# Output projection in 24 tiles of 344 columns instead of 16 groups of 2 x 258, and some steps in another place

## What is computed

```python
hn = rmsnorm(h, norm_mix)
z = hn @ w_in                                    # 1024 -> 3584
u_in, c_gate, b_gate, q, k, v, g = split(z)
y_conv = b_gate * causal_conv3(c_gate * u_in, conv_w)
o, ret_state = retention(rotary(q), rotary(k) * QK_DIM ** -0.5, v)   # chunks of 128, 4 heads
y_ret = head_rmsnorm(o) * silu(g)
h = h + concat([y_conv, y_ret]) @ w_out          # output projection, 1024 -> 1024
hn2 = rmsnorm(h, norm_mlp)
h = h + square(relu(hn2 @ w_up)) @ w_down        # 1024 -> 4096 -> 1024
y = rmsnorm(h, norm_final)
```

## Time and profile before

| | us |
|---|---|
| median of 3 runs | 1154.47 |
| lowest, highest | 1154.11, 1156.49 |
| the profiled execution | 1154.86 |
| its span, first to last instruction | 1153.1 |
| PE busy | 1141.2 (99%) |
| DVE, POOL, ACT busy | 769.6, 557.7, 442.2 |
| output projection, first matmul to first of the next stage | 389.48 to 481.90 |

### The profile page before, as it was taken

One profiled execution on the slowest core, in us unless ns is written; L12 is line 12 of the kernel. 1 busy time (PEld: TensorE's weight loads), 2 busy tenths in 40 slices (PEclk: granted clock), 3 DMA queues, 4 the chain that ended last, 5 costly groups with the idle time before them and its releaser, 6 DMA issues.

```text
span 1153.1 us, 22631 instructions
## 1 busy us (share of the span) xinstructions
PE 1141.2 (99%) x8685; PEld 1120.0 (97%) x8685; DVE 769.6 (67%) x1147; ACT 442.2 (38%) x915; POOL 557.7 (48%) x540
## 2 busy tenths in 40 slices
PE   9999999999999999999999999999999999999996
PEld 7899999999999999999999999999999999999996
DVE  4355546456455576689777777776878777777856
ACT  6422413413324433453333333334553443544414
POOL 0154233252251240124233242322899899999992
PEclk9999999999999999999999999999999999999998
DMA  6431221311202042154534435336972544454314
GB/s 205 133 109 40 60 72 42 88 54 37 84 29 57 30 137 84 47 150 169 182 116 147 148 123 182 111 130 228 298 253 88 183 148 133 144 185 147 93 38 147
DMA packets 154296, 139.79 MB, mean 121 GB/s; under 512 B 6842, under 2 KB 118179, under 8 KB 154205
## 3 DMA queue, kind: packets, MB, share of 16 engines
q1 hardware_dynamic: 149071, 135.50, 36.8%
q10 hardware_dynamic: 5134, 3.05, 0.9%
HBM read 98.07 MB, written 40.47 MB: 120 GB/s over the span
## 4 chain that ended last, share of the span: by engine, by line
PE 97%; DMA 1%; DVE 1%; issue 0%; ACT 0%; SPq 0%; DVEq 0%; ACTq 0%
PE pair L1911 19%; PE pair L1912 18%; PE pair L1913 18%; PE pair L1695 8%; PE pair L1697 8%; PE pair L1696 8%; PE pair L1888 3%; PE pair L1890 3%; PE pair L1889 3%; PE pair L1754 1%; PE pair L1755 1%; PE pair L1757 1%; PE pair L1805 1%; PE pair L1800 1%; PE pair L1814 1%; PE pair L1802 1%
## 5 line engine op out<-in xcount | busy, mean ns | idle before, releaser
L1911 PE MATMUL pair<-m_hi,dn_hi 128*128 128x258 f32 (+2 forms) x896 | 255.3, 285 | 0.4 <-DVE hid L1663 0.3
L1911 PE MATMUL pair<-b_hi,up_hi 128*128 128x258 f32 x896 | 254.8, 284 | 0.0
L1912 PE MATMUL pair<-b_lo,up_hi 128*128 128x258 f32 x896 | 253.6, 283 | 0.0
L1912 PE MATMUL pair<-m_lo,dn_hi 128*128 128x258 f32 (+2 forms) x896 | 253.6, 283 | 0.0
L1913 PE MATMUL pair<-m_hi,dn_lo 128*128 128x258 f32 (+2 forms) x896 | 253.3, 283 | 0.0
L1913 PE MATMUL pair<-b_hi,up_lo 128*128 128x258 f32 x896 | 252.1, 281 | 0.0
L1695 PE MATMUL pair<-x_hi,w_both 128*128 128x344 f32 (+2 forms) x576 | 188.8, 328 | 0.0
L1697 PE MATMUL pair<-x_hi,w_both 128*128 128x344 f32 (+2 forms) x576 | 184.3, 320 | 0.0
L1696 PE MATMUL pair<-x_lo,w_both 128*128 128x344 f32 (+2 forms) x576 | 184.2, 320 | 0.0
L1663 DVE TENSOR_TENSOR hid<-pair,hid 128x516 f32<-128x516 f32 (+2 forms) x194 | 124.6, 642 | 76.4 <-PE pair L1913 74.3
L1911 PEld LDWEIGHTS pair<-b_hi,up_hi 128*128 128x128 f32 x896 | 169.2, 189 | 2.0 <-issue 0.2
(11 more groups left out here) (214 smaller groups left out, 2167.8 us busy)
## 6 DMA issues: line engine op xcount, KB each, us to landing
m_raw<-m_dram SPq DMA_DIRECT2D x56, 516.0 KB, 4.8
m_dram<-hid SPq DMA_DIRECT2D x64, 258.0 KB, 2.8
up_raw<-w_up_dram SPq DMA_DIRECT2D x32, 512.0 KB, 5.0
dn_raw<-w_down_dram SPq DMA_DIRECT2D x128, 128.0 KB, 2.4
w_raw<-w_in_dram SPq DMA_DIRECT2D x28, 512.0 KB, 3.7
m_dram<-hid SPq DMA_DIRECT2D x16, 774.0 KB, 4.0
h_dram<-hid SPq DMA_DIRECT2D x8, 516.0 KB, 3.1
h_in<-h_dram SPq DMA_DIRECT2D x16, 258.0 KB, 5.8
```

Of the source, the lines that this page charges most:

```text
L1911: m_.matmul(to, shs[k], mhs[k], start=STARTS[i] and k == 0, stop=False, skip_group_check=more)
L1912: m_.matmul(to, shs[k], mls[k], start=False, stop=False, skip_group_check=more)
```

## The change

The 16 groups become 24 tiles, three for each output block (`TILE_OUT`), each of 344 columns in a single bank; six banks (0 to 5) are used in turn. Tile 1 of a block crosses the border of the two halves of columns. Everything that counted groups counts tiles: `h_done` and `main_done`, and the waits on them. `tiles_of(gi)` gives the number of tiles that must be read before the steps of half-group gi. `out_read` adds one bank of 344 columns. `y_low` counts each of its pieces, and the first two tiles wait for the pieces one by one. DVE's order at the last block changes: the two `up_low` that stood before the last read stand before the last but one. Some steps elsewhere are moved: ACT's `m_hi` of products 5 and 6 in block 0 of MLP down; `scaled(LASTU, 3)` on DVE and `squared(LASTU, 3)` on ACT by one product; three parameter loads from ACT's queue to SP's; the meta rows in one load; one warm-up matmul fewer; the last store on ACT's queue.

```diff
+TILE_OUT = [(n, t) for n in range(KT) for t in ((0, 1, 2) if n < 4 else (2, 1, 0))]
+TILES = len(TILE_OUT)
...
-MID_HIGH = ({11: 0, 13: 1, 15: 2, 17: 3, 20: 4, 22: 5, 24: 6}, {4: 0, 6: 1, 8: 2, 12: 3, 15: 4, 19: 5, 22: 6})
+MID_HIGH = ({11: 0, 13: 1, 15: 2, 17: 3, 20: 4, 21: 5, 22: 6}, {4: 0, 6: 1, 8: 2, 12: 3, 15: 4, 19: 5, 22: 6})
...
-WARM = (8, 3)
+WARM = (7, 3)
...
-        def out_pair(gi):
-
-            return pair[gi % 3 if gi < 12 else 3 if gi == 12 else (gi - 1) % 3]
+        def tiles_of(gi):
+
+            return 3 * (gi // 2) + 2 + gi % 2
...
             load_v(3)
+            sp.dma_start(prm_raw[GMLP:GMLP + KT, :], io["norm_mlp"].rearrange("l (k p) -> (l k) p", p=P)).then_inc(prm_in, 16)
+            sp.dma_start(prm_raw[CW:CW + 12, :], io["conv_w"].rearrange("l r (c p) -> (l r c) p", p=P)).then_inc(prm_in, 16)
+            sp.dma_start(prm_raw[CACHE:PROWS, :], io["cache_conv"].rearrange("l b r (c p) -> (l b r c) p", p=P)).then_inc(prm_in, 16)
             load_x(1)
...
-                    for part in range(2):
-                        sp.wait_ge(f_ready, i + 1 + part)
-                        sp.dma_start(io["y_prompt"][0, r0:r0 + n, CH * part:CH * part + CH], y[0:n, CH * part:CH * part + CH]).then_inc(y_stored[i % 4], 16)
+                    sp.dma_start(io["y_prompt"][0, r0:r0 + n, 0:CH], y[0:n, 0:CH]).then_inc(y_stored[i % 4], 16)
...
-            act.dma_start(x_raw[0:META, 0, 0:CH], meta[:, 0:CH]).then_inc(x_half, 16)
+            act.dma_start(x_raw[0:META, 0, :], meta).then_inc(x_half, 16)
...
-                    if q == 0 and i == 5:
+                    if q == 0 and i == 6:
                         squared(LASTU, 3)
...
+            END = len(FINAL) - 1
+            l, c0, c1 = FINAL[END]
+            act.wait_ge(f_ready, END + 2)
+            act.dma_start(io["y_prompt"][0, HALF * l + c0:HALF * l + c1, CH:D], y_out[END % 4][0:c1 - c0, CH:D]).then_inc(y_stored[END % 4], 16)
...
-                    ins = d.tensor_tensor(y_lo[:, k0:k1, c0:c1], y_raw[:, k0:k1, c0:c1], y_hi[:, k0:k1, l, :], ALU.subtract)
-                ins.then_inc(ylo_done, 1)
+                    d.tensor_tensor(y_lo[:, k0:k1, c0:c1], y_raw[:, k0:k1, c0:c1], y_hi[:, k0:k1, l, :], ALU.subtract).then_inc(ylo_done, 1)
...
+                if gi % 2 == 0:
+                    out_read(3 * n)
+                if gi == 14:
                     up_low(0, 0)
                     up_low(0, 1)
-                out_read(gi)
+                out_read(tiles_of(gi) - 1)
...
-                    if q == 0 and i == 4:
+                    if q == 0 and i == 5:
                         scaled(LASTU, 3)
...
-            def out_group(gi):
+            def out_tile(j):
+
+                n, t = TILE_OUT[j]
+                c0, c1 = START[t], START[t] + TW
                 pe.wait_ge(w_ready, U_OUT + n + 1)
+                if j < 3:
+                    pe.wait_ge(main_read, G_OUT - 2 + j)
+                elif j == 3:
+                    pe.wait_ge(o_read, 9 * HEADS)
+                elif j < 6:
+                    pe.wait_ge(y_ready, 3 * HEADS + 3)
                 else:
-                    pe.wait_ge(h_done, gi - 2)
+                    pe.wait_ge(h_done, j - 5)
+                to = bank[j % 6][:, 0:TW]
+                for idx, k in enumerate(K_ORDER):
+                    if j < 2 and idx in (0, HEADS - 1, KT - 1):
+                        pe.wait_ge(ylo_done, 3 * j + (0, HEADS - 1, KT - 1).index(idx) + 1)
```

More of the change, by code:

```diff
@@ L748, in _ @@
             pool.wait_ge(main_done, G_OUT)
-            pool.wait_ge(ylo_done, 4)
+            pool.wait_ge(ylo_done, 6)
             for n in range(KT):
@@ L755, in _ @@
                 up_sum(0, i)
-            pool.wait_ge(main_done, G_OUT + GROUPS)
+            pool.wait_ge(main_done, G_OUT + TILES)
             up_sum(0, 3)
@@ L979, in square @@
                 n, l = SEQ_OUT[gi]
-                act.wait_ge(h_done, gi + 1)
+                act.wait_ge(h_done, tiles_of(gi))
                 if gi == 0:
@@ L1384, in halves, with out_read @@
                 return x.rearrange("p (t c) -> p t c", c=TQ)
-            def out_read(gi):
-                n, l = SEQ_OUT[gi]
-                dve.wait_ge(main_done, G_OUT + gi + 1)
+            def out_read(j):
+                n, t = TILE_OUT[j]
+                dve.wait_ge(main_done, G_OUT + j + 1)
                 dve.wait_ge(xs_done, n + 1)
-                hc = halves(hid_half(n, l))
-                d.tensor_tensor(hc, out_pair(gi)[:, :, 0:TQ], hc, ALU.add).then_inc(h_done, 1)
+                hc = hid[:, n, START[t]:START[t] + TW]
+                d.tensor_tensor(hc, bank[j % 6][:, 0:TW], hc, ALU.add).then_inc(h_done, 1)
             def square_sum(gi):
@@ L1863, in _ @@
             ins.then_inc(ctailT_done, 1)
-            def out_group(gi):
-                n, l = SEQ_OUT[gi]
-                c0, _ = cols(l)
+            def out_tile(j):
+                n, t = TILE_OUT[j]
+                c0, c1 = START[t], START[t] + TW
                 pe.wait_ge(w_ready, U_OUT + n + 1)
[L1871 to L1878, removed]
-                else:
-                    pe.wait_ge(h_done, gi - 2)
[L1881 to L1888, removed]
-                        m_.matmul(to, sh, ml, start=False, stop=False)
-                        ins = m_.matmul(to, sl, mh, start=False, stop=idx == KT - 1)
@@ new lines, in out_tile @@
+                if j < 3:
[4 more added lines that the diff above has]
+                    pe.wait_ge(y_ready, 3 * HEADS + 3)
+                else:
+                    pe.wait_ge(h_done, j - 5)
[3 more added lines that the diff above has]
+                        pe.wait_ge(ylo_done, 3 * j + (0, HEADS - 1, KT - 1).index(idx) + 1)
+                    sh, sl = w_hi[:, n % 2, P * k:P * k + P], w_lo[:, n % 2, P * k:P * k + P]
+                    mh, ml = y_hi[:, k, :, :].rearrange("p l c -> p (l c)")[:, c0 - META:c1 - META], y_lo[:, k, c0:c1]
+                    m_.matmul(to, sh, mh, start=idx == 0, stop=False)
+                    m_.matmul(to, sh, ml, start=False, stop=False)
+                    ins = m_.matmul(to, sl, mh, start=False, stop=idx == KT - 1)
@@ L1901, in row_sums @@
                 ins.then_inc(sum_done, 1)
-            for gi in range(GROUPS):
-                out_group(gi)
+            for j in range(TILES):
+                out_tile(j)
             def product(to, shs, sls, mhs, mls, i):
@@ L1937, in _ @@
                         if i == 1:
-                            pe.wait_ge(h_done, GROUPS - 1)
+                            pe.wait_ge(h_done, TILES - 2)
                         if i == 4:
-                            pe.wait_ge(h_done, GROUPS)
+                            pe.wait_ge(h_done, TILES)
                     for t in range(2):
```

22 lines of the change are left out of this document (9 added, 13 removed).

## The result

| | kernel before | changed kernel |
|---|---|---|
| median of 6 runs each, us | 1154.25 | 1158.86 |
| lowest, highest | 1153.43, 1156.49 | 1158.22, 1161.78 |
| the profiled execution | 1154.86 | 1158.62 |
| its span, mean granted clock | 1153.1, 0.997 | 1156.7, 0.994 |

The ratio is 1.0044, with a 95% interval of 1.003 to 1.0059: the change costs 4.6 us by the medians. The forecast was 1159.2, slower.

What follows compares the result with a forecast made beforehand. PE was taken as the bound, busy 1141.2 of 1153.1 us with a queue of matmuls. The terms -1.6 - 0.5 + 0.15 + 4.9 + 2.0 - 0.2 gave +4.75 us, 1159.2 beside the median; range 1156.5 to 1161.9.

Steps and rivals of the forecast that it cites:

- 1 pitch of the output projection: Output projection: 576 matmuls of 344 columns at 157.6 ns replace 768 of 258 at 120.3 ns; -1.6 us.
- 2 into the stage; the second tile's wait: Output projection's start: first tile needs only y_lo's first piece, -0.5 us; second tile waits for a late piece, +0.15.
- 3 out of the stage: Output projection's end: last sum of squares still ready 0.25 us ahead of PE's row sums; 0, up to 0.4 allowed.
- 4 the stop, less the one that goes: Down projection block 0: a1 copy waits behind m_raw 5's load, PE 5.4 us late, less a 0.44 us stop; +4.9.
- 5 the clock: Behind that stop PE's clock falls to half rate for about 4 us; +2.0 us.
- 6 the start: Kernel start: moved loads and one warm-up matmul fewer change nothing, as the first weight load keeps its place; 0.
- 7 the end: Kernel end: last half row's store issued by ACT, not by SP behind the first half's; -0.2 us.
- Rival (d): Output projection: the 344-column pitch, read in another stage, gains nothing here; 1160.8 us, within the main case, no own chance.
- E: Start of the first up matmul after the output projection, the zero for the forecast times in term 3.
- Rival (a): Down projection: the stop comes without the fall of the clock; 1157.2 us, chance 0.28.
- Rival (b): Down projection: m_raw 5's load is there when ACT asks, no stop, only gains; 1151.9 us, chance 0.07.

Runs made afterwards that it cites:

- start_only: Kernel before with only the new start (one meta load, three parameter loads on SP, one warm-up matmul fewer): 1154.48 us, ratio 1.0001.
- table_only: Kernel before with only the new table of m_hi splits (products 5 and 6 at steps 21 and 22): 1160.52 us, ratio 1.0052.
- fill_stop: Changed kernel with 18 added matmuls on ones into an unused bank, keeping PE busy while it waits for the a1 copy: 1158.00 us, ratio 1.0031.
- mid_first: Changed kernel with SP issuing the loads of m_raw 5 and 6 ahead of the fourth group's h_in loads: 1155.13 us, ratio 1.0003.
- a1_first: Changed kernel, new table kept, with ACT's a1 copy placed ahead of the m_hi split of the same step: 1153.68 us, ratio 0.9995.
- table_back: Changed kernel with the old table of m_hi splits (products 5 and 6 at steps 22 and 24): 1153.61 us, ratio 0.9989.
- tiles_only: Kernel before with only the new output projection in tiles of 344 columns; old table, start, last unit and tail: 1152.86 us, ratio 0.9984.

## Why the prediction was right

The spans differ by 1156.7 - 1153.1 = 3.6 us. Part by part, forecast and measured in the two traces:

| part | forecast | measured |
|---|---|---|
| 1 pitch of the output projection | -1.6 | -1.70 |
| 2 into the stage; the second tile's wait | -0.5; +0.15 | -0.63; +0.19 |
| 3 out of the stage | 0 | 0 |
| 4 the stop, less the one that goes | +4.9 | +4.5 less 0.44, and +0.19 at another stop |
| 5 the clock | +2.0 | +2.65 |
| 6 the start | 0 | -0.88 in this trace, none by start_only |
| 7 the end | -0.2 | -0.27 in this trace |
| sum | +4.75 | +3.6 |

**1.** The pitch read in the input projection held in the output projection: 157.5 ns against 157.6. The line through the two widths gave 8.4 ns for each matmul beside its columns; 1.70 us for 192 matmuls fewer is 8.9. The estimate by the 2.5 ns of the Trainium skill (TensorE: Matmul & The Clock Gate, "Back-to-back issue gap"), 0.5 us, did not hold against the measured 1.7. That section calls its formula the gap of an isolated matmul and says that in a stream of weight loads and matmuls both set the spacing; each matmul here has its own weight load, so the figure was not made for this sum. Rival (d) falls with it.

**2.** Both sizes held, and so did the reason for the small wait: PE stopped at the second tile, at 393.09.

**3.** The last read stood at E + 0.73 (forecast 0.7), the end of the last sum at E + 2.64 (2.65), PE at E + 2.88. The cover of 0.25 us was there.

**4.** The mechanism is shown by three kernels: the table alone brings the stop, taking it back or putting the copy first removes it. The size was 0.9 us too large. The step that failed is "the load is issued at 841.46 ... none of this is moved": I kept the load's delay against PE as in the trace of before. It was wanted by PE's third product at 840.0 and landed at 842.7, 2.7 us later, where before these were 842.67 and 846.23, 3.6 us apart: 0.9 us less, the size of the error. The load was issued 3.2 us sooner while PE was 2.7 us ahead, and took 4.42 us instead of 4.77. In table_only the stop had 5.35 us, so what I forecast is within what occurs. Of that kind is also the 0.19 us at 814.78.

**5.** The fall of the clock was read from the tail, and came in the stop; fill_stop shows that it is PE's idleness that brings it. The phase was longer than I took, 27 matmuls, and 14 in the other trace, 2.65 and 1.4 us; 2.0 lies between. Nor does the one delay read from the tail, 2.0 to 2.5 us, hold: from PE's last work to the fall it was 3.4 us in this stop, 4.7 in that of table_only and 3.1 in that of mid_first. That 2.0 came near is thus in part luck. The Trainium skill (the same page, "HAM oscillation") warns of this pattern, and here the rows agree: 1.00 until 843.0, 0.50 from 844.5 on (the windows above). Rival (a), the stop without the clock, is refuted in the trace; by the medians it is 1.2 us that separate it, less than the trace's 2.65 and not clear of the spread.

**6 and 7.** The forecast of 0 for the start was right for the code and not for this trace; the difference is chance. The same goes for the end: PE's end to the end of the span is 8.61 us before and 8.34 after, but 8.23 in table_only, where the old tail stands. The store on ACT's queue does what it says; the trace of the changed kernel shows the two issues overlapping in time, 0.77 and then 0.36 us, where the earlier trace rows had 1.70:

```profile
1151.88 0.77 SPq L644 DMA_DIRECT2D y_prompt_dram<-y_out  x1
1152.54 0.36 ACTq L1175 DMA_DIRECT2D y_prompt_dram<-y_out  x1
```

A gain from it can't be told from the spread. So the forecast's 1159.2 against 1158.86 is closer than its parts: part 4 was 0.6 us too large, part 5 0.65 too small, and the medians of the two kernels stand 4.6 us apart where their profiled executions stand 3.8 apart.

**Rival (b)**, the load landed in time, would have meant 1151.9. It is what a1_first brings about in another way; there 1153.7 was measured. Some 0.8 us lies between a1_first or table_back and tiles_only, which I can't settle; the intervals of their ratios overlap. In their traces steps of 0.4 to 0.8 us stand in block 0 of the down projection, at other places in each, behind DVE in table_back, behind ACT and POOL in tiles_only, others with no engine named. None of the kernels isolates them, and the moved square and scale of the last up unit and the last store were not timed alone. Nor is it known why two of the changed kernel's runs took 1161.1 and 1161.8 us with the same mean clock of 0.994 as the others.

## What to carry to other kernels

On an engine that takes its instructions in order, the wait for a DMA belongs behind every copy that frees a buffer for the busy engine; an instruction moved one step ahead costs nothing of its own and all of what its wait holds up. Ask of each moved step which semaphore it waits for, when that comes by the trace, and what stands right behind it. A stage of many equal matmuls could be priced here by two pitches, read at two widths in two stages, and an early start of a whole trace is proof of nothing before other kernels with the same code show it.

## What the runs showed of the hardware

The clock fell after a stop of only 2.05 us (PE's idle time) in mid_first, and not in the stop: the window from 842.5 to 843 is full (1.00) with PE working again, the one from 843 to 844 has 0.70, the next 0.50. So a stop can be over before its price begins. In the changed kernel the fall, at about 843.6, came within the stop, and the clock came back at about 850.4, after some 6 us of unbroken work at half rate; in table_only it fell at about 846.7, 4.7 us after PE had stopped, and came back at about 850.1, after 3 us of work.

A matmul of 344 columns costs 157.5 ns and one of 258 120.3 ns from start to start, each with a load of new weights: 0.43 ns a column and 8 to 9 ns beside them, between these two widths.

The load of `m_raw` 5 took 4.42 us from issue to landing in the changed kernel, with the `h_in` loads ahead of it (3.7 to 4.8 in the traces of before, table_only, fill_stop and a1_first), and 6.31 us in mid_first, when issued 4 us sooner, ahead of them and behind `dn_raw` loads. The DMA share was 0.9 to 1.2 all this time, and the earlier issue bought only some 2 us of its 4.
